# First mix of a three-layer float32 network: a fourth raw buffer, another order of weight splits and convolution taps, the norm in two halves, four convolution products moved from TensorE to VectorE

## The reference

```python
h = rms_norm(x, norm1_g)
q, k, v, u = split(h @ w_in)              # w_in: 1024 x 2560; q, k, v 512 wide, u 1024
q, k = rope(rms_norm(q)), rope(rms_norm(k))   # 8 heads of 64
attn = softmax(q k^T / 8, causal) v
a, g = split(u + glu_b)                   # 512 channels each
c = a * sigmoid(g)
c = depthwise causal convolution of c over tokens, 31 taps, + dw_b
conv = silu(layer_norm(c) * ln_g + ln_b)
x = x + concat(attn, conv) @ w_out        # w_out: 1024 x 1024
```

## Time and profile before

| | |
|---|---|
| median of 3 runs | 1287.15 us (1286.68 to 1287.18) |
| the profiled execution | 1286.3 us, its span 1284.5 us |
| granted PE clock, mean | 0.998 |
| PE busy | 1275.7 us, 99% of the span |
| PEld, DVE, ACT, POOL busy | 1091.4, 837.8, 676.7, 119.9 us |
| moved by DMA | 234.96 MB, mean 183 GB/s |

### The profile page before, as it was taken

How to read it: one execution, slowest core, us unless ns; L and a number is a source line. 1 busy time by engine, 2 the same in 40 slices (tenths; PEclk the granted TensorE clock), 3 DMA queues, 4 the chain that set the end, 5 groups by cost and what they waited for, 6 DMA issues and landing times.

```text
span 1284.5 us, 18324 instructions
## 1 busy us (share of the span) xinstructions
PE 1275.7 (99%) x7092; PEld 1091.4 (85%) x7092; DVE 837.8 (65%) x1102; ACT 676.7 (53%) x904; POOL 119.9 (9%) x135
## 2 busy tenths in 40 slices
PE   9999999999999999999999999999999999999998
PEld 8978888888888888887888888888888877888886
DVE  6997655565655548898765556655565776675552
ACT  6876554443544435656564444544454665564441
POOL 4860000000000000022000000000002120000000
PEclk9999999999999999999999999999999999999999
DMA  9526765563765553527565554675553755475530
GB/s 282 172 83 194 252 209 196 196 212 119 242 200 187 186 153 119 177 85 244 197 230 182 185 190 162 201 258 196 194 186 127 242 160 165 150 238 186 184 144 33
DMA packets 174352, 234.96 MB, mean 183 GB/s; under 512 B 4352, under 2 KB 154128, under 8 KB 174289
## 3 DMA queue, kind: packets, MB, share of 16 engines
q1 hardware_dynamic: 170368, 223.52, 52.9%
q0 software_dynamic: 3184, 9.37, 2.4%
q10 hardware_dynamic: 736, 1.19, 0.3%
HBM read 233.03 MB, written 1.05 MB: 182 GB/s over the span
## 4 chain that ended last, share of the span: by engine, by line
PE 93%; POOL 2%; DVE 2%; ACT 1%; issue 1%; DMA 0%; DVEq 0%; SPq 0%; POOLq 0%; ACTq 0%
PE psum L1225 23%; PE psum L1121 15%; PE psum L1122 14%; PE psum L1123 14%; PE psum L1233 12%; PE psum L1246 2%; PE psum L1188 2%; PE psum L1187 2%; PE psum L1186 2%; POOL ws L1042 2%; PE psum L1250 1%; PE psum L1457 1%; PE psum L1348 1%; PE psum L1505 1%; PE psum L1470 1%
## 5 line engine op out<-in xcount | busy, mean ns | idle before, releaser
L1892 DVE TENSOR_TENSOR w_lo<-raw,w_hi 128x2048 fp32r<-128x2048 f32 (+1 forms) x200 | 457.7, 2294 | 86.1 <-ACT w_hi L473 84.7
L473 ACT ACTIVATE w_hi<-raw 128x2048 fp32r<-128x2048 f32 (+1 forms) x212 | 403.5, 1907 | 35.5 <-PE psum L1123 13.7
L1225 PE MATMUL psum<-t_both,w_hi 128*128 128x512 f32 x1280 | 304.8, 390 | 0.0
L1225 PEld LDWEIGHTS psum<-t_both,w_hi 128*128 128x128 f32 x1280 | 237.4, 188 | 47.4
L1121 PE MATMUL psum<-w_hi,f_hi 128*128 128x512 f32 x488 | 192.8, 395 | 0.0
L1123 PE MATMUL psum<-w_hi,f_lo 128*128 128x512 f32 x488 | 190.2, 390 | 0.0
L1122 PE MATMUL psum<-w_lo,f_hi 128*128 128x512 f32 x488 | 190.1, 389 | 0.0
L1121 PE MATMUL psum<-w_hi,t_both 128*128 128x512 f32 (+2 forms) x464 | 165.8, 357 | 0.1
L1123 PE MATMUL psum<-w_hi,t_both 128*128 128x512 f32 (+2 forms) x464 | 162.4, 350 | 0.0
L1122 PE MATMUL psum<-w_lo,t_both 128*128 128x512 f32 (+2 forms) x464 | 162.2, 350 | 0.0
L1233 PEld LDWEIGHTS psum<-t_both,w_lo 128*128 128x128 f32 x1280 | 158.8, 192 | 3.1
(11 more groups left out here) (217 smaller groups left out, 1296.2 us busy)
## 6 DMA issues: line engine op xcount, KB each, us to landing
raw<-in_ffn_wg SPq DMA_DIRECT2D x44, 1024.0 KB, 5.6
raw<-in_ffn_wu SPq DMA_DIRECT2D x44, 1024.0 KB, 5.4
raw<-in_ffn_wd SPq DMA_DIRECT2D x44, 1024.0 KB, 5.1
raw<-in_even_w_in SPq DMA_DIRECT2D x12, 1024.0 KB, 5.3
raw<-in_odd_w_in SPq DMA_DIRECT2D x12, 1024.0 KB, 5.3
raw<-in_w_gate SPq DMA_DIRECT2D x11, 1024.0 KB, 5.5
raw<-in_w_up SPq DMA_DIRECT2D x11, 1024.0 KB, 5.4
raw<-in_w_down SPq DMA_DIRECT2D x11, 1024.0 KB, 5.0
```

Source lines behind the costliest of these rows:

```text
L473: nc.scalar.activation(w_hi[:, n % SLOTS, 0:w], raw[:, n % RAWS, 0:w], ACT.Copy).then_inc(hi_done, 1)
L1225: mm = nc.tensor.matmul(bank[b + c][:, :], wh[:, k, c * P:(c + 1) * P], t_both[:, k, :, :].rearrange("p a s -> p (a s)"), start=k == 0 and ...
L1892: nc.vector.tensor_tensor(w_lo[:, n % SLOTS, 0:w], raw[:, n % RAWS, 0:w], w_hi[:, n % SLOTS, 0:w].bitcast(F32), ALU.subtract).then_inc(lo_ ...
```

## The change

- **A fourth raw buffer for one unit.** Unit 3 (`SPARE`) lands in 2048 words of the workspace at word 6008, which hold scratch of the input norm before and keys and queries later. Its load waits for the normed input (`xn_ready` 4) in place of the low part of unit 0. Units 4, 5 and 6 wait for the low parts of units 0, 1 and 2 (before: 1, 2, 3); from unit 7 on each wait is as it was. All later units lie one raw buffer lower.
- **Order on ACT.** A sigmoid on one number (which makes ACT load that table) and the high part of unit 2 stand ahead of the parameter copies; high parts of units 3 to 6 stand earlier among the gates and taps.
- **Order on DVE.** The four lambda products move from the setup (before the low part of unit 2) to behind the low part of unit 6, and their table's load is awaited there. The low parts of units 3 to 5 stand one place earlier; 20 taps stand ahead of the first mean square, where 11 stood.
- **Four products from PE to DVE.** Taps 27 to 30 of tile 2 are DVE's now: 62 taps on DVE, 11 on PE. DVE's list begins with 13 taps of tile 0, and now has neighbours of one tile. PE's three pieces of tile 3 stand one place later (at steps 13, 14, 15; before 12 to 15), and POOL builds three sets of diagonals and not four. DVE's last run of taps has 3 where it had 8.
- **The norm in halves.** Taking off the mean and squaring are two instructions each, of two tiles each; PE's mean begins with tile 1 and waits for each tile by itself; the variance begins when the first two tiles are squared and goes to another bank.

```diff
+        raw_spare = wv(6008, UNIT)
+        SPARE = RAWS
+        def raw_of(n):
+            return raw_spare if n == SPARE else raw[:, (n - (n > SPARE)) % RAWS, :]
+        def raw_landed(n):
+            m = n - (n > SPARE)
+            return (spare_in, 16) if n == SPARE else (raw_in[m % RAWS], 16 * (m // RAWS + 1))
...
-        PE_TAPS = {ACT_PE: range(20, TAPS), DVE_PE: range(27, TAPS)}
-        PIECES = [(ct, tap, min(tap + 4, TAPS)) for ct in (ACT_PE, DVE_PE) for tap in range(PE_TAPS[ct].start, TAPS, 4)]
-        DVE_TAPS = [(tap, 0) for tap in range(11)]
-        for n in (3, 2, 5, 3, 2, 2, 9, 5, 3, 5, 8):
-            for i in range(n):
-                ct = 0 if i % 2 else 2
-                DVE_TAPS.append((sum(c == ct for _, c in DVE_TAPS), ct))
+        PE_TAPS = range(20, TAPS)
+        PIECES = [(tap, min(tap + 4, TAPS)) for tap in range(PE_TAPS.start, TAPS, 4)]
+        DVE_TAPS = []
+        for ct in map(int, "0000000000000" "2022022" "202" "20" "20202" "202" "20" "20" "202022022" "20220" "202" "20220" "202"):
+            DVE_TAPS.append((sum(c == ct for _, c in DVE_TAPS), ct))
...
SP:
-                if n >= RAWS:
-                    sp.wait_ge(lo_done, n - RAWS + 1 + SLOTS * turn)
+                if n == SPARE:
+                    sp.wait_ge(xn_ready, 2 * T)
+                elif n > SPARE:
+                    sp.wait_ge(lo_done, n - RAWS + (n > 2 * RAWS) + SLOTS * turn)
...
ACT:
                     split_to(2)
+                    nc.scalar.activation(st[:, 150:151], st[:, 2:3], ACT.Sigmoid)
+                    split_to(3)
                     act.wait_ge(params_T, 2)
...
-                split_to(3)
+                split_to(4)
                 gate(0)
-                split_to(4)
-                taps(2)
                 split_to(5)
-                taps(2)
+                taps(4)
+                split_to(6)
                 gate(2)
                 taps(2)
-                split_to(6)
-                taps(2)
                 split_to(7)
-                taps(3)
+                taps(5)
                 square(4)
...
-                act.wait_ge(cen_ok, 1)
-                nc.scalar.activation(V["sq"], V["acc"], ACT.Square).then_inc(sq4_ok, 1)
-                act.wait_ge(sq4_ok, 1)
+                for g in range(2):
+                    act.wait_ge(cen_ok, g + 1)
+                    cts = slice(2 * g, 2 * g + 2)
+                    nc.scalar.activation(V["sq"][:, cts, :], V["acc"][:, cts, :], ACT.Square).then_inc(sq4_ok, 1)
+                act.wait_ge(sq4_ok, 2)
...
POOL:
                     build(1)
-                    add(1)
-                    build(1)
-                    add(3)
+                    add(4)
...
PE:
-                    if i >= 12:
-                        conv(i - 12)
+                    if i >= 13:
+                        conv(i - 13)
...
-                pe.wait_ge(conv_ok, 2)
-                pe.wait_ge(side_ok, 1)
-                for ct in range(4):
-                    mm = nc.tensor.matmul(bank[4][:, 0:S], mean_w[:, :], V["acc"][:, ct, :], start=ct == 0, stop=ct == 3)
+                for ct in (1, 0, 2, 3):
+                    if ct == 1:
+                        pe.wait_ge(tap_added, TAPS - 1)
+                    elif ct == 0:
+                        pe.wait_ge(conv_ok, 1)
+                    elif ct == 2:
+                        pe.wait_ge(side_ok, 1)
+                    mm = nc.tensor.matmul(bank[4][:, 0:S], mean_w[:, :], V["acc"][:, ct, :], start=ct == 1, stop=ct == 3)
...
-                pe.wait_ge(sq4_ok, 1)
                 for t in range(T):
                     for ct in range(4):
-                        mm = nc.tensor.matmul(bank[4][:, S + t:S + t + 1], V["sq"][:, ct, t * P:(t + 1) * P], mean_w[:, 0:1],
+                        if t == 0 and ct % 2 == 0:
+                            pe.wait_ge(sq4_ok, ct // 2 + 1)
+                        mm = nc.tensor.matmul(bank[5][:, S + t:S + t + 1], V["sq"][:, ct, t * P:(t + 1) * P], mean_w[:, 0:1],
...
DVE:
                 dve.wait_ge(params_ok, 2)
+                split_to(4)
                 glu(1)
-                split_to(4)
-                taps(2)
                 split_to(5)
-                taps(9)
+                taps(7)
                 split_to(6)
+                taps(6)
                 glu(3)
                 split_to(7)
+                lam_sums()
+                taps(7)
                 mean_square(0)
...
                 group_sums(L, 4)
-                taps(8)
+                taps(3)
...
-                nc.vector.tensor_tensor(V["acc"], V["acc"], bank[4][:, 0:S].unsqueeze(1).broadcast_to([P, 4, S]), ALU.subtract)\
-                    .then_inc(cen_ok, 1)
+                for g in range(2):
+                    cts = slice(2 * g, 2 * g + 2)
+                    nc.vector.tensor_tensor(V["acc"][:, cts, :], V["acc"][:, cts, :], bank[4][:, 0:S].unsqueeze(1).broadcast_to([P, 2, S]), ALU.subtract)\
+                        .then_inc(cen_ok, 1)
```

More of the change, by code:

```diff
@@ L238, in build @@
         raw_in = [sem(f"raw_in{i}") for i in range(RAWS)]
+        spare_in = sem("spare_in")
         half_in = sem("half_in")
@@ L467, in split_hi @@
             def split_hi(n, width=UC, turn=0):
-                act.wait_ge(raw_in[n % RAWS], 16 * (n // RAWS + 1) + turn * (16 * SLOTS // RAWS))
+                landed, count = raw_landed(n)
+                act.wait_ge(landed, count + turn * (16 * SLOTS // RAWS))
                 if n >= SLOTS:
@@ L472, in split_hi @@
                 w = KT * width
-                nc.scalar.activation(w_hi[:, n % SLOTS, 0:w], raw[:, n % RAWS, 0:w], ACT.Copy).then_inc(hi_done, 1)
+                nc.scalar.activation(w_hi[:, n % SLOTS, 0:w], raw_of(n)[:, 0:w], ACT.Copy).then_inc(hi_done, 1)
             def split_to(n):
@@ L1051, in build @@
                                 pool.wait_ge(piece_done, p - 1)
-                            ct, lo, hi = PIECES[p]
+                            lo, hi = PIECES[p]
                             shape = [P, hi - lo, P]
@@ L1780, in conv @@
                         pe.wait_ge(nmax_ok, L["h0"] + 4)
-                    ct, lo, hi = PIECES[p]
+                    lo, hi = PIECES[p]
                     for tap in range(lo, hi):
-                        mm = nc.tensor.matmul(bank[3][:, (ct - 2) * S:(ct - 1) * S], V["diag"][:, 4 * (p % 2) + tap - lo, :],
-                                              V["hpad"][:, ct, tap:tap + S], start=tap == PE_TAPS[ct].start, stop=tap == TAPS - 1)
+                        mm = nc.tensor.matmul(bank[3][:, 0:S], V["diag"][:, 4 * (p % 2) + tap - lo, :],
+                                              V["hpad"][:, ACT_PE, tap:tap + S], start=tap == PE_TAPS.start, stop=tap == TAPS - 1)
                     mm.then_inc(piece_done, 1)
@@ L2188, in mix_first, with lam_sums @@
                 roots = seen[id(rstd_ready)]
-                dve.wait_ge(setup_in[2], 16 * 2)
+                def lam_sums():
+                    dve.wait_ge(setup_in[2], 16 * 3)
+                    for i in range(2):
+                        ins = nc.vector.tensor_tensor_reduce(out=lam_in[:, 128 * i:128 * i + 64], in0=lam_in[:, 128 * i:128 * i + 64],
+                                                             in1=lam_in[:, 128 * i + 64:128 * i + 128], scale=1.0, scalar=0.0,
+                                                             op0=ALU.mult, op1=ALU.add, accum_out=st[:, 20 + i:21 + i])
+                    ins.then_inc(lam_sum, 1)
                 def taps(n):
@@ L2313, in mix_first @@
                 dve.wait_ge(var_ok, 1)
[L2314 removed]
+                nc.vector.tensor_scalar(st[:, 10:12], bank[5][:, S:S + T], EPS, None, ALU.add).then_inc(ms_ready, 1)
                 nx(rstd_ready, 5)
                 dve.wait_ge(spread_ok, 1)
[L2317 removed]
+                dve.wait_ge(cen_ok, 2)
                 for g in range(2):
@@ L2555, in setup @@
                 dve.wait_ge(ident_in, 16)
-                dve.wait_ge(setup_in[1], 16 * 4)
-                for i in range(2):
-                    ins = nc.vector.tensor_tensor_reduce(out=f_s[:, i, 0:64], in0=lam_in[:, 128 * i:128 * i + 64],
-                                                         in1=lam_in[:, 128 * i + 64:128 * i + 128], scale=1.0, scalar=0.0,
-                                                         op0=ALU.mult, op1=ALU.add, accum_out=st[:, 20 + i:21 + i])
-                ins.then_inc(lam_sum, 1)
+                dve.wait_ge(setup_in[1], 16 * 3)
                 for i in range(2):
```

18 lines of the change are left out of this document (8 added, 10 removed).

## The result

| | before | changed |
|---|---|---|
| median of the runs shown | 1287.09 us (1285.63 to 1289.10, 22 runs) | 1289.01 us (1288.21 to 1290.09, 22 runs) |
| the profiled execution, its span | 1286.3, 1284.5 us | 1288.88, 1287.0 us |

The ratio is 1.0015, with a 95% interval of 1.0009 to 1.0020: the change costs 1.9 us, between 1.2 and 2.6. The forecast was +0.5 us with its own range to +2.7: the direction and the range held, the size was too small.

The account below looks back on a forecast made before the run. DVE's order was taken as the bound, with PE just beside it: +0.8 us (DVE's lag at head 6) + 0 (products) - 0.3 (squares) = +0.5 us, forecast 1287.6 us; range for 8 in 10 1285.5 to 1289.6 us.

Parts of the forecast that it names:

- DVE's order is the clock: From some 40 us on, DVE's own order sets the time, with PE running just ahead or just behind it.
- Four products off PE are worth 0: Before head 4, PE's 1.89 us of spared work becomes slack spent waiting for ACT's exponentials; gain 0.
- 3.0 us filled: Of DVE's 3.7 us of fillable waits from 14 to 50 us, new taps fill all but 0.7 us.
- 0.3 us given back by POOL: Low parts of units 5 to 7 lost 2.0 us while POOL was adding; 0.3 us of it returns to DVE.
- 0.4 us more for neighbours: DVE's later tap runs before head 6 have three neighbours of one tile, costing 3 x 0.12 = 0.4 us.
- 0.4 less for `group_scale`: DVE waited 0.40 us more for ACT at `group_scale`; a late DVE fills this also.
- The halves: At the variance, the first half square ends earlier and PE's wait goes; gain 0.2 to 0.4 us, taken as 0.3.
- PE's short waits near 60 and 63 us: PE waits briefly for DVE at unit 8's low part and unit 6's rotated half, coming 0.6 us late to head 4.
- PE as the path: Faster rival: head 4's exponentials and head 6's maxima come early, PE gains 2.9 us, 1284.2 us; chance 0.07 in full.
- The lock: Slower rival: low parts of units 2 to 6 each lose 1.1 us to POOL; +5.1 us, 1292.2 us; chance 0.05.
- Colliding first loads: Slower rival: unit 3's early data delays POOL's small tables and DVE's setup; +3.5 us, 1290.6 us; chance 0.04.
- the extra buffer does nothing: Rival: landings don't move and about 1.9 us more of DVE's waits stay; +2.4 us, 1289.5 us; chance 0.08.

Follow-up runs that it names:

- late_taps: The changed kernel with seven of DVE's taps moved from before the first mean square to the last run; 1286.91 us, ratio 1.0003.
- products_back: The changed kernel with the four products on PE again and DVE's list four taps shorter; 1287.34 us, ratio 1.0005.
- products_late: The kernel before with the four products moved to DVE, at the end of its last run; 1286.97 us, ratio 1.0001.
- spare_late: The changed kernel with unit 3's load waiting for the low part of unit 0, as before; 1289.98 us, ratio 1.0025.
- early_only: The changed kernel with the four products on PE and without the seven early taps; 1287.06 us, ratio 1.0000.
- late_conv12: The changed kernel with seven taps moved to DVE's last run and PE's three pieces one step earlier; 1287.61 us, ratio 1.0000.
- gate_first: The changed kernel with `gate(0)` ahead of unit 3's high part on ACT; 1288.71 us, ratio 1.0012.
- gate_first_late: The changed kernel with seven taps moved to DVE's last run and `gate(0)` ahead of unit 3's high part on ACT; 1285.87 us, ratio 0.9988.
- loads_only: The kernel before with the fourth buffer and its earlier loads alone; 1287.07 us, ratio 1.0000.
- halves_only: The kernel before with the norm in halves and nothing else; 1285.35 us, ratio 0.9991.
- loads_halves: The kernel before with the fourth buffer, its load rules and the norm in halves, products and orders as before; 1285.69 us, ratio 0.9988.

## Why the prediction was right in its mechanism and off in its size

**DVE's order is the clock: right.** `values(4)` followed the first mean square at a nearly fixed distance (45.3 to 45.8 us) in all kernels, and seven taps moved behind it gave back 2.1 us (late_taps), four 1.7 us (products_back, where the products went back to PE too).

**Four products off PE are worth 0: right.** products_back put them back and lost nothing by it, products_late took them off at no gain. The slack turned into waits before `values(2)` and `turn(4)`, as foretold, 0.79 and 1.04 us.

**"3.0 us filled": the step that failed.** The prediction left 1.0 us for unit 1 and 0.7 us for the rest of DVE's early waits, 1.7 us; 0.2 and 3.6 us were measured, 3.8 together. Of the 4.7 us of the earlier trace rows 0.8 us was filled (4.66 to 3.82), and the 0.4 us for POOL's root among these lay behind the first mean square. The lambda table, PE's unit 1 and POOL's root are waited for no more, but waits for ACT's high parts rose from 2.3 to 3.8 us: 0.96 us for unit 2 (0 to 0.3 foretold), 1.79 for unit 3 (0 to 1), 0.86 for unit 4 (none). The word "filled" misled. DVE works in order, its four waits end at 27.36 us, and the first of the 20 taps begins at 29.57 us: no tap stands ahead of a wait, so none could fill one. The waits could shrink only if the data came earlier. For that the prediction had unit 3 land 9 to 11 us after its issue, from a load that was issued near 15 us, when the dip to 86 GB/s was about to come. Here it lay behind units 1 and 2 in a full queue. It took 11.1 us, just over the upper bound (10.17 + 11.1 = 21.3 us); in the other kernels with the early load it took 10.5 to 13.2 us, 12.2 or more in six of nine. "Unit 4's data and all later ones then come before they are asked for" was wrong too: unit 4 landed at 25.3 us after 1.33 us of waiting.

The sum with what was measured, in the trace's own time. From start to next start the taps before the first mean square take 3.60 + 3.01 + 3.06 = 9.7 us instead of 0.97 + 4.60 = 5.6: 4.1 us more, as foretold. The waits ahead of it fell from 4.2 to 3.8 us: 0.4 less. The low parts of units 5 and 6 are quicker by (2.69 - 2.28) + (2.80 - 2.44) = 0.8 us. The lambda products take 0.84 us at their new place (41.65 to 42.49) and took 0.30 at the old one (19.18 to 19.48): 0.5 more, which the prediction did not have. That is 4.1 - 0.4 - 0.8 + 0.5 = 3.4 us; the trace says 45.55 - 42.32 = 3.2. The prediction's 0.3 us given back by POOL came out, but by luck, as 0.8 less 0.5. To head 6 0.4 us is made up (foretold 0.4 us more for neighbours and 0.4 less for `group_scale`, so 0), to 88.61 - 85.76 = 2.85 us, where 0.8 was foretold. The halves take off 0.4, and the profiled execution is 2.6 us longer. Counted from A, which is 0.55 us later in it, the same three are 2.7, 2.3 and, at Z, 2.0 us; the median is 1.9 us higher.

**The halves: right, slightly more.** 0.38 us for 0.3, and PE starts the variance behind the output's rows without a wait, at 101.55 us.

**Missed: PE's bank.** The prediction looked for PE's short waits near 60 and 63 us, at low part and rotated half; PE had none there. They were at 47.74 and 55.35 us, where units 6 and 7 want the bank that DVE's rotation of units 4 and 5 frees. Both rotations stand in DVE's order behind the seven new taps. It named what PE reads from DVE, not what PE writes over. **Missed: `gate(0)`**, for which PE waited 2.9 us in spare_late's profiled execution, 2.2 in early_only's and 1.8 in late_conv12's. In the changed kernel's it was nothing, and gate_first says that it is not what makes that median; with the taps late it costs 1.0 us (gate_first_late).

**The rivals.** PE as the path is refuted by products_back. The lock is there, but not at the price that the rival put on it: of the low parts of units 2 to 6 four took 2.28 or 2.29 us and one 2.44; only unit 7's took 3.38, as before. What it does shows on POOL's side. These are POOL's additions that met a low part, one that met none (31.28 us), and the first lambda product on DVE, all of the changed kernel:

```profile
28.22 2.03 POOL L1054 TENSOR_TENSOR ws<-ws 128x256 f32<-128x256 f32 x1 [4.80 <-ACT ws L730]
31.28 0.74 POOL L1054 TENSOR_TENSOR ws<-ws 128x256 f32<-128x256 f32 x1
33.80 2.25 POOL L1054 TENSOR_TENSOR ws<-ws 128x256 f32<-128x256 f32 x1 [1.78 <-ACT ws L730]
39.72 2.61 POOL L1054 TENSOR_TENSOR ws<-ws 128x256 f32<-128x256 f32 x1
49.15 1.56 POOL L1057 TENSOR_TENSOR ws<-ws 128x512 f32<-128x512 f32 x1
41.65 0.76 DVE L2212 CUSTOM_DVE_ANT_0 ws<-ws 128x64 f32<-128x64 f32 x1
```

Whoever began first went through, and the other waited. The low parts of units 4, 5 and 6 ended at 29.65, 35.45 and 41.73 us, and the additions begun during them ended 0.60 us behind each, after 2.03, 2.25 and 2.61 us instead of 0.74. Unit 7's low part (49.48 us) began during the addition of 49.15 us and ended at 52.86 us, 2.29 us behind a point 0.14 us before that addition's end; those of units 5 and 6 before (36.09 and 39.59 us) fit the same way. The lambda product began during the addition of 39.72 us and took 0.76 us where the one before took 0.22. The rule of the Trainium skill, "SBUF — State Buffer", section "Who interferes with whom", by which such a pair holds each other up for whole instructions, agrees with this trace. So the rival's price, 1.1 us at each low part, fails because most low parts began first, and the cost went to POOL. Colliding first loads are refuted in the form that was meant: DVE's low part of unit 2 ended at 19.21 + 2.29 = 21.5 us, where 21.9 was expected. That the extra buffer does nothing was priced at +2.4 us, and +1.9 is near it, but spare_late shows that the early load does carry 1.0 us of the changed kernel's time, in whose order ACT asks for unit 3 early; in the old order (loads_only) nothing can be told. The truth is between: the landing moved by 2.7 us (24.05 to 21.3), the issue by nearly 5.

**Two differences that the timeline explains in part.** halves_only is 1.5 us lower in the median and 0.5 us at Z. The executions lie in clumps: of the 34 of the kernel before beside it, 8 lie between 1285.4 and 1286.1 us, 22 between 1286.3 and 1287.9 and 4 near 1289.0; of the 11 of halves_only 9 lie between 1285.1 and 1286.1. The lowest moved by 0.3 us only (1285.43 to 1285.14), as the timeline has it; the rest of the 1.5 is that more executions fell into the lowest clump. Why they did stays open, and the same holds of loads_halves and gate_first_late, whose lowest are 1284.98 and 1285.21 us.

PE's bracketed waits grew from 0.96 to 4.03 us, by 3.1, in the first mix (without `mean_w`, the same in both) while its work fell by 1.89: that explains 1.2 of the 1.99 us at Z. Of the other 0.8 us some 0.5 is in what a bracket leaves out. A unit's products start every 0.12 us, though each is shown as 0.28 us long. At the first bank wait the starts go 47.09, 47.74, 47.96 us, where two steps would take 0.24 us: 0.63 us are lost, and the bracket says 0.37. The two bank waits so cost 0.5 us beyond their 1.54, and in the 15 us from 45.55 us PE did 111 products where it had done 128 in the 15 us from 45 us: 17 x 0.12 = 2.0 us. The last 0.3 us stays open.

## What to carry to other kernels

In an in-order engine new work fills a wait only if it stands ahead of it. Work that stands behind the waits is paid for only if what ends the waits comes earlier; first find whether the last link, here the data of a load, moves with the change. A load issued earlier lands earlier only by what the queue had idle. And a wait moved ahead in an in-order engine holds all that stands behind it: list who needs those steps, banks to be freed as well as operands, before the wait is priced at nothing.

## What the runs showed of the hardware that was not expected

A 1 MB load issued at 9.8 to 11.3 us, behind two others, took 10.5 to 13.2 us to land, by execution, while the transfers ran at about 350 GB/s. A stretch of 2.86 us without products was followed by a granted clock of 0.50 until some 32 us (spare_late): from 28 to 30 us PE did 12 products, where 19 fit at full clock. So that stall cost PE more than its length; after the 2.21 us of early_only the clock stayed at 1.00. And a DVE instruction that reads two operands from SBUF and an addition on POOL ran one after the other, whichever began first: 0.74 us of POOL's became 2.03 to 2.61, and 2.29 us of DVE's up to 3.38.
